# Spreading the sample-state units of a retention mixer evenly over its projection steps, with the first read moved inside a step

## The reference, cut to what matters

```
q, k, v, g = split(h @ w_in)              # w_in: 1024 x 6144
q, k = rotary(q), rotary(k) * DK**-0.5
S[b, h] = gamma[h] * S[b, h] + outer(k[b, h], v[b, h])   # 8 x 4 states
o[b, h] = q[b, h] @ S[b, h]
o = groupnorm(o) * silu(g);  return o @ w_out
```

## Time and profile before

| what | us |
| --- | --- |
| median of 3 runs | 1741.76 |
| lowest and highest run | 1740.02, 1741.95 |
| the profiled execution's own time | 1741.48 |
| its span in the trace | 1739.6 |
| TensorE busy | 1622.3 (93%) |
| VectorE, ScalarE, GpSimd busy | 751.5, 382.1, 97.6 |

### The profile page before, as it was taken

How to read it: one execution, slowest core, us unless ns; L and a number is a source line. 1 busy time by engine, 2 the same in 40 slices (tenths; PEclk the granted TensorE clock), 3 DMA queues, 4 the chain that set the end, 5 groups by cost and what they waited for, 6 DMA issues and landing times. The chain is left out here.

```text
span 1739.6 us, 29551 instructions
## 1 busy us (share of the span) xinstructions
PE 1622.3 (93%) x11480; PEld 1091.0 (63%) x11480; DVE 751.5 (43%) x1860; ACT 382.1 (22%) x804; POOL 97.6 (6%) x118
## 2 busy tenths in 40 slices
PE   7998899999999999999998899989999999999996
PEld 4776665777566555565665587766656566566563
DVE  2204435216644435435345235357553534534435
ACT  2012343112211112112112336231111211112112
POOL 0000110000000000000000001011000000000000
PEclk9999899999999999999999899999999999999998
DMA  9994599338999999999997784688999999999970
GB/s 368 384 369 169 204 395 403 115 141 331 421 419 420 421 419 417 420 420 413 420 419 307 248 263 139 244 328 331 421 420 420 421 420 420 418 418 416 418 323 26
DMA packets 154111, 603.96 MB, mean 347 GB/s; under 512 B 18253, under 2 KB 63473, under 8 KB 101690
## 3 DMA queue, kind: packets, MB, share of 16 engines
q1 hardware_dynamic: 137354, 559.89, 81.0%
q0 software_dynamic: 16064, 40.92, 6.2%
q10 hardware_dynamic: 624, 2.23, 0.3%
HBM read 594.42 MB, written 26.90 MB: 357 GB/s over the span
## 5 line engine op out<-in xcount | busy, mean ns | idle before, releaser
L2269 PE MATMUL ps<-ring,scratch 128*64 128x256 f32 x4352 | 485.3, 382 | 26.2 <-DMA ring<-in_moe_w_up 24.4
L2269 PEld LDWEIGHTS ps<-ring,scratch 128*64 128x64 f32 x4352 | 333.7, 138 | 164.8 <-issue 37.1
L2301 PE MATMUL ps<-ring,scratch 128*64 128x512 f32 x1088 | 243.6, 598 | 3.5 <-DVE scratch L2625 1.8
L2250 PE MATMUL ps<-scratch 128*128 128x264 bf16 x1632 | 196.6, 277 | 4.5 <-issue 4.1
L2595 DVE SCALAR_TENSOR_TENSOR scratch<-scratch,ps 128x256 f32<-128x256 f32 x68 | 32.7, 482 | 381.9 <-ACT scratch L2709 381.8
L734 PE MATMUL ps<-hT,ring 128*128 128x264 f32 x768 | 183.4, 396 | 1.3 <-ACT hT L371 1.3
L2250 PEld LDWEIGHTS ps<-scratch 128*128 128x128 bf16 x1632 | 141.9, 97 | 63.6 <-issue 19.7
L734 PEld LDWEIGHTS ps<-hT,ring 128*128 128x128 f32 x768 | 149.6, 196 | 30.3 <-issue 1.6
L2301 PEld LDWEIGHTS ps<-ring,scratch 128*64 128x64 f32 x1088 | 70.6, 136 | 148.8 <-issue 104.1
L2566 DVE TENSOR_TENSOR scratch<-scratch,ps 128x264 f32<-128x264 f32 x256 | 109.9, 429 | 57.8 <-PE ps L2250 57.8
L2709 ACT ACTIVATE scratch<-ps 128x256 f32<-128x256 f32 x68 | 26.2, 385 | 482.5 <-PE ps L2269 482.5
(11 more groups left out here) (345 smaller groups left out, 1320.8 us busy)
## 6 DMA issues: line engine op xcount, KB each, us to landing
ring<-in_moe_w_gate SPq DMA_DIRECT2D x136, 1024.0 KB, 18.6
ring<-in_moe_w_up SPq DMA_DIRECT2D x136, 1024.0 KB, 17.8
ring<-in_moe_w_down SPq DMA_DIRECT2D x136, 1024.0 KB
ring<-in_ada_w SPq DMA_DIRECT2D x48, 1024.0 KB, 12.8
ring<-in_ret_w_in SPq DMA_DIRECT2D x24, 1024.0 KB, 16.7
ring<-in_state_ret SPq DMA_DIRECT2D x16, 1024.0 KB, 15.2
out_ret_sample<-ring POOLq DMA_DIRECT2D x16, 1024.0 KB, 9.0
ring<-in_gla_w_in SPq DMA_DIRECT2D x12, 1024.0 KB, 11.9
```

Of the source, the lines that this page charges most:

```text
L2250: mm = nc.tensor.matmul(k.ps[:, c % 2, 0:T], row_parts[:, p, s, c * P:(c + 1) * P], slot_token[:, p, :], start=(p == 0 and s == 0), stop=( ...
L2269: mm = nc.tensor.matmul(k.ps[lo:lo + CAP, 2 + p, j * DE:(j + 1) * DE], xg[:, p, c, lo:lo + CAP], slot(k, n, DE)[:, c, :], start=(c == 0), ...
L2301: mm = nc.tensor.matmul(k.ps[lo:lo + CAP, 6 + half, :], hid_t[:, p, m, lo:lo + CAP], slot(k, n, D)[:, m, half * 512:(half + 1) * 512], sta ...
```

## The change

Units are given to steps by one table, two to each of the steps 12 to 15 and three to each of the steps 16 to 23 (before: none in step 12, two in 13 and 14, four in 15, then two or four in turn). `STATES_AT`, and with it the order of the loads, follows. On TensorE the units stand in the middle of the halves. The first read moves from the end of step 16 to the middle of it, and sample 1 is read at its end. VectorE updates the units of a query step ahead of the rotation. Head 3's values are prepared in the middle of step 12, the other heads' products in the middle of steps 9 to 11. Before step 16 TensorE waits only for the seventh rotation, and for the eighth before step 17's first gate.

```diff
-SAMPLES_HEAD_AFTER = {9: 0, 10: 1, 11: 2, 12: 3}
-STATES_AT = {13: [0], 14: [1], 15: [2, 3], 16: [4], 17: [5, 6], 18: [7], 19: [8, 9], 20: [10], 21: [11, 12], 22: [13],
-             23: [14, 15]}
-READS_AT = {16: [0], 17: [1], 18: [2], 19: [3], 21: [4], 22: [5], 23: [6]}
+SAMPLES_HEAD_AT = {9: 0, 10: 1, 11: 2, 12: 3}
+UNITS_FROM = {12: 0, 13: 2, 14: 4, 15: 6, 16: 8, 17: 11, 18: 14, 19: 17, 20: 20, 21: 23, 22: 26, 23: 29, 24: 32}
+STATES_AT = {t: range((UNITS_FROM[t] + 1) // 2, (UNITS_FROM[t + 1] + 1) // 2) for t in range(12, 24)}
+READS_MID = {16: [0]}
+READS_AT = {16: [1], 18: [2], 19: [3], 20: [4], 22: [5], 23: [6]}
...
     def units_at(t):
-        return [2 * i + j for i in STATES_AT.get(t, []) for j in range(2)]
+        return range(UNITS_FROM[t], UNITS_FROM[t + 1]) if t in STATES_AT else []
...
                 us = units_at(t)
-                for u in us[:len(us) // 2]:
+                for u in us[0:1]:
                     spread_value(u)
                 project(t, 0, 2 * (t % 2), first.s_h if t == 0 else None)
-                for u in us[len(us) // 2:3]:
+                if t in SAMPLES_HEAD_AT:
+                    sample_values(SAMPLES_HEAD_AT[t])
+                for u in us[1:2]:
                     spread_value(u)
                 project(t, 1, 2 * (t % 2) + 1).then_inc(k.ring_free[loads[t] % RING], 1)
-                for u in us[3:]:
-                    spread_value(u)
...
-                if t in SAMPLES_HEAD_AFTER:
-                    sample_values(SAMPLES_HEAD_AFTER[t])
-
-            pe.wait_ge(s_qk, 8)
+
+            pe.wait_ge(s_rot, 7)
             for t in range(first_gate, last_step + 1):
                 wait_slot(k, pe, loads[t])
                 us = units_at(t)
-                for u in us[0::4]:
-                    spread_value(u)
+                spread_value(us[0])
                 for m in range(2):
                     n = 2 * (t - first_gate) + m
                     if n >= 4:
                         pe.wait_ge(s_sil, n - 3)
-                    mm = project(t, m, gate_bank(n))
-                    for u in us[m + 1::4]:
-                        spread_value(u)
-                    if m:
-                        mm.then_inc(k.ring_free[loads[t] % RING], 1)
-                for u in us[3::4]:
-                    spread_value(u)
+                    elif n == 2:
+                        pe.wait_ge(s_qk, 8)
+                    pause = (5, 3)[m]
+                    project(t, m, gate_bank(n), chunks=range(pause))
+                    spread_value(us[m + 1])
+                    mm = project(t, m, gate_bank(n), chunks=range(pause, DC))
+                    if m == 0:
+                        for b in READS_MID.get(t, []):
+                            read(b)
+                mm.then_inc(k.ring_free[loads[t] % RING], 1)
...
@@ vector
+                if t in SAMPLES_HEAD_AT:
+                    place_values(SAMPLES_HEAD_AT[t])
+                    split_values(SAMPLES_HEAD_AT[t])
+                for u in units_at(t):
+                    update(u)
                 if t < 4 or t >= 12:
                     rotate(t)
-                if t in SAMPLES_HEAD_AFTER:
-                    place_values(SAMPLES_HEAD_AFTER[t])
-                    split_values(SAMPLES_HEAD_AFTER[t])
                 if t == 12:
                     nc.vector.memset(qz, 0.0).then_inc(s_qz, 1)
-                for u in units_at(t):
-                    update(u)
@@ scalar
             for t in range(16):
+                if t == 12:
+                    samples_out(SAMPLES_HEAD_AT[t])
                 for u in units_at(t):
                     outers(u)
...
             for t in range(first_gate, last_step + 1):
-                us = units_at(t)
-                for u in us[0:2]:
+                for u in units_at(t):
                     outers(u)
                 wait_used(k, act, loads[t])
...
-                for u in us[2:4]:
-                    outers(u)
```

More of the change, by code:

```diff
@@ L727, in transposes, with project @@
                 cond_transpose(k, k.ps[:, bank], rows[:, g % 2]).then_inc(s_crt, 1)
-            def project(t, m, bank, chunk_ready=None):
+            def project(t, m, bank, chunk_ready=None, chunks=range(DC)):
                 w = slot(k, loads[t], 256)
-                for c in range(DC):
+                for c in chunks:
                     if chunk_ready:
@@ L1144, in _, with samples_out @@
             first.modulate(act)
+            def samples_out(h):
+                act.wait_ge(s_v3t, h + 1)
+                nc.scalar.copy(vs[0:COPIES, h * RDV:(h + 1) * RDV], k.ps[0:COPIES, 6, :]).then_inc(s_v3c, 1)
             for t in range(16):
+                if t == 12:
+                    samples_out(SAMPLES_HEAD_AT[t])
                 for u in units_at(t):
@@ L1154, in _ @@
                     rows_out(CONDITION_AFTER[t])
[L1155 to L1158, removed]
+                if t < 12 and t in SAMPLES_HEAD_AT:
+                    samples_out(SAMPLES_HEAD_AT[t])
             for t in range(first_gate, last_step + 1):
-                us = units_at(t)
-                for u in us[0:2]:
+                for u in units_at(t):
                     outers(u)
```

## The result

The changed kernel takes 1724.63 us (median of 4 runs, 1722.73 to 1726.09), the kernel before 1741.69 us (median of 4); the ratio is 0.9904 with a 95% interval of 0.9888 to 0.9919. That is 17.1 us less. The forecast was 1724 us, 17.4 us less.

The account below looks back on a forecast made before the run. Bound by TensorE's waits on VectorE's order and a load queue stalled until `read(0)`, then by full DMA. TensorE alone saves 24.3 us; 6.6 us of weight waits and 0.3 of clock leave 17.4: 1741.5 to 1724 us, range 1716 to 1732.

Parts of the forecast that it names:

- The waits for ScalarE and head 3 go; clock 1.00: TensorE, steps 12 to 16: 13.0 us of outer-product waits and 2.7 us for value rows vanish; full clock 150 to 177 us.
- TensorE alone would need 24.3 us less: Steps 12 to 23 counted by TensorE's work alone: 106.0 us, so `scores` starts at 246.1 instead of 270.36 us.
- Moved transposes 0.0 to 0.3 us each, taken as 0: Transposes moved into steps 10 and 11 meet the previous head's split at nearly the same moment; cost counted as 0.
- Release at 176.8 us: SyncE's load queue, held until `read(0)` ends, goes on at 176.8 us, 23.0 us earlier than at 199.78.
- Step 23's weights 66.3 us after the release: Load queue: 23.5 loads and stores at 2.82 us per MB come first, so these weights land at 243.1 us.
- 6.6 us of waits at steps 21 to 23: TensorE wants step 23's weights at 236.5 us, they land at 243.1; the wait is shared by three step starts.
- 0.3 us for the clock: Allowance, from a range of 0 to 2.6 us, for TensorE's clock falling in the waits for weights.
- `scores` at 253.0 us: Start of attention after step 23 and its read, 17.4 us earlier than before.
- the queue does not bind: Rival: loads come quicker than 2.82 us or stores give way, so all 24.3 us are gained; 1717 us, chance 0.15.
- given back later: Rival: output projection or experts wait for something with its own clock, so the time stays 1741 us; chance 0.06.
- the slower case: Rival: the dense stretch behind one release runs DMA below TensorE's need; 1747 us at 3.8 us per MB, chance 0.08.
- The gate wait: Before step 16, TensorE waiting only for the seventh rotation; without this edit, step 15's rotation would cost its 2.3 us.

Follow-up runs that it names:

- weights_ahead_ends: weights_ahead with the sample-value transposes of heads 0 to 2 back at the ends of steps 9 to 11; 1716.88 us.
- rotation_first: The changed kernel, but VectorE rotates before it updates the units, as in the kernel before; 1728.14 us.
- gate_wait_all: The changed kernel, but TensorE waits for all eight rotations before step 16, as in the kernel before; 1725.26 us.
- read_at_step_end: The changed kernel, but sample 0 is read at the end of step 16 and not in its middle; 1731.57 us.
- half_stores: The changed kernel with only the first head of each pair of sample states stored, output incomplete; 1715.49 us.
- weights_ahead: The changed kernel with another load order alone: weights of steps 13 to 16 ahead of S0, of 17 to 20 ahead of later states; 1717.83 us.

## Why the prediction was right

Step by step, times from L456 where two kernels are compared. The mechanism is the one forecast. The size is so in part by luck: the forecast has 17.4 us in this part, the profiles show 15.6, and the medians differ by 17.1 because another 1.5 us lie outside the stretch, within what differs from run to run.

- *The waits for ScalarE and head 3 go; clock 1.00.* Right: none of them is left, and the clock is 1.00 up to 219 us.
- *TensorE alone would need 24.3 us less.* Right: where the queue has slack (weights_ahead_ends) the stretch is 23.7 us less.
- *Moved transposes 0.0 to 0.3 us each, taken as 0.* Too low: step 11's transposes come at 138.06 us, 8.00 us after those of 130.06 where an unhindered period is 7.56 us, and the same in step 10: 0.8 us in all. The split and the copy of the next head's values end later than the middle of the step. Moving them to the ends gave 1.1 us.
- *Release at 176.8 us.* 178.99, of which 1.1 is an early part that began later in this profile (L456 at 118.33 and 117.22 us; the ten other profiles have 117.1 to 117.4 or 118.1 to 118.5), 0.8 the transposes.
- *Step 23's weights 66.3 us after the release.* 244.50 - 179.09 = 65.4 us. Counting megabytes of loads and stores, at the 2.82 us each that the kernel before showed, held within 1 us; in rotation_first and gate_wait_all it is 65.8 and 65.6 us, in read_at_step_end 67.5. The Trainium skill ("DMA: Bandwidth & Descriptors", Bandwidth) has about 358 GB/s as the limit on the HBM side for this direction, and says in the same section that one core alone gets more. The rows after, of one core, show 394 to 403 GB/s under full load; they agree with the latter.
- *6.6 us of waits at steps 21 to 23.* 5.0 us, at just these three steps; the late release and transposes had moved TensorE's need too.
- *0.3 us for the clock.* Too low: step 23 took 9.57 us from its first spread to its read (244.50 to 254.07 us), where step 22 at full clock took 7.9, so 1.7 us. The forecast reasoned that a wait of 2.67 us was not followed by slow products and longer ones were. But the kernel before also has a shorter one, followed by the slow read of 247.45 us that the forecast itself counts (1.6 us):

```profile
247.15 0.38 PE L753 MATMUL ps<-scratch,pick 96*128 96x512 bf16 x1 [2.29 <-ACT rstd L1138]
```

- *`scores` at 253.0 us.* 255.91 = 253.0 + 1.1 (early part) + 0.8 (transposes) + 0.2 (rest up to the release) - 0.9 (landing) + 1.4 (clock) + 0.3 left over. The errors partly cancel.
- *A first experts stage 17 us earlier.* 14.5 us in the profiles, 15.6 from L456; right in kind, less in size.

Of the rivals, "the queue does not bind" falls with half_stores and weights_ahead, which each give the 7 us that it would have had; "given back later" falls with the third column of the table; the slower case needed 3.57 us per megabyte, and 2.78 were seen (65.4 us over 23.5).

The gate wait was called worth its 2.3 us if undone. In the changed kernel step 23 started 2.7 us later and the stretch lost 1.0, since the low clock after the last wait, 1.7 us, happened to stay away; in the version without waits for weights the stretch lost 2.5. The term was right.

## What to carry to other kernels

When a ring of slots is loaded in a fixed order, find the piece that waits for the longest-held slot, and count the megabytes (stores too) from its release to each later deadline: that count gave the landing within 1.2 us in four kernels (65.4 to 67.5 us, forecast 66.3), and it also says which pieces to move ahead of the holder. An engine's list that puts a wait for the end of a step ahead of work that doesn't need it stalls the others most when the units are bunched; spread evenly, the order was worth 4 us, and 10 where they were bunched. Where the loads are counted from a release, a wait ahead of it is not hidden by later waits for these loads: the gate wait moved step 23 by 2.7 us. And after each new order of loads, look again for the piece that holds the queue: the place of the read was worth 7 us where `read(0)` held it, and nothing where the end of step 16 did (weights_ahead_ends).

## What was not expected of the hardware

The granted clock doesn't follow the length of one wait alone. Waits of 2.67 us, of 2.36 us (before step 16 in gate_wait_all) and of 2.22 and 2.05 us (before step 23 in rotation_first and gate_wait_all) were followed by product records at full pace. One of 2.33 us before step 23 of the changed kernel was followed by 10 records in 3.47 us instead of 2.39, at a mean granted clock of 0.76 in 244.5 to 251.5 us, and cost 1.7 us by the end of the step; one of 2.29 us in the kernel before was followed by a read of 3.47 us instead of 1.90. What tells these waits apart wasn't tried. And a load of 1 MB under full DMA took 23.9 us to land in read_at_step_end, where the slowest in the kernel before took 20.0 and in the changed kernel 21.5; what made it slow is open.
